# Scaling the inputs of the unit sums behind the root (second feed-forward) and in front of it (first), in a macaron block of 512 tokens on one core

## The chip, the cores and the metric

The kernel runs on one core of one Trainium2 chip. The metric is the device time of one launch in microseconds (us); less is better. The core has five engines with instruction streams of their own: TensorE (PE, matmuls; its weight loads are PEld), VectorE (DVE), ScalarE (ACT), GpSimd (POOL) and SyncE (SP, which here only issues transfers). They wait for each other through semaphores. Two on-chip memories matter: SBUF, and PSUM, into which TensorE writes.

## The reference

One layer in float32 on x of 512 tokens by 1024 features:

```
x = x + 0.5 * swiglu(rms_norm(x, ffn1_norm), ffn1_gate, ffn1_up, ffn1_down)
x = x + hybrid_mixer(rms_norm(x, mix_norm), ...)      # linear attention, differential attention, short convolution
x = x + 0.5 * swiglu(rms_norm(x, ffn2_norm), ffn2_gate, ffn2_up, ffn2_down)
out = rms_norm(x, final_norm)

rms_norm(x, g) = x * rsqrt(mean(x*x) + eps) * g
swiglu(h, wg, wu, wd) = (silu(h @ wg) * (h @ wu)) @ wd      # 1024 -> 2816 -> 1024
```

## The kernel before

**Layout and precision.** x lies with features on partitions, as KT = 8 tiles of 128 features by 512 tokens. Each matmul of float32 accuracy is three matmuls (`three`, L570): operands are split into a high part (`_hi`, written by ScalarE, `split_hi`, L1106) and a remainder (`_lo`, written by VectorE, `split_lo`, L1486, a subtraction of two SBUF operands), and hi x hi, hi x lo and lo x hi are added up. The rms factor is applied after the products: the matmuls work on x * gain, and the result is multiplied by `rinv`.

**Feed-forward.** The 2816 hidden features are 22 tiles (FT). The first four (PLAIN) are computed by plain products: `pair(m)` is a gate product and an up product, each of one weight slab of 128 x 1024 and 24 matmuls of 512 columns. The other 18 are "units" which use a Strassen-like scheme: seven block products of 256 columns on sums of weight quarters and on sums of activation quarters. The sums of the weights are GpSimd's, one unit after the other (`sums`, L483). The sums of the activations are made once per feed-forward, also by GpSimd (`activation_sums`, L505): six TENSOR_TENSOR instructions of 128 x 1024 on `xg`. `xg` is x * gain in plain float32, eight tiles written by ScalarE (`scaled_x`, L1125). ScalarE and VectorE then split the sums into `s_hi` and `s_lo`, in pair 2 and pair 3, and the first unit's products read them. `xg`, the sums and the squares of the start lie in parts of the array `h` that are not yet in use.

**The root.** For the norm, PE adds up the squares (`mean_squares`, L594, four small matmuls), ScalarE takes the square root (`root`, L1157), VectorE inverts it (`invert`, L1514: a reciprocal of four columns and four TENSOR_SCALARs of 128 columns that put it on the diagonal of `rinv`), PE spreads it over the partitions (`spread_rms`, L602, waits for `diag_ready`), and ScalarE copies the result from PSUM to `rinv` (`copy_rms`, L1161). In the first feed-forward (f = 0) the mean squares stand behind pair 1's gate product and the spread in the middle of pair 1's up product (`spread_at`, L630). In the second (f = 1) the mean squares stand between the two products of pair 0, and the spread behind them.

**Order.** Each engine's program is written out by hand; it runs in order and stops at the first wait that isn't met. In ScalarE's `pair(0)` stand: splits, the root, another split, the scalings of `xg` (k from 0 in the second feed-forward, from 4 in the first, where 0 to 3 stand ahead of `ffn_up`), the copy of the rms, then the wait for VectorE's first gate product and the Silu. In VectorE's `pair(0)` stand a split, the inversion, another split, then the wait for `rinv`, and the gate product. GpSimd's `activation_sums` begins with a wait for all eight tiles of `xg` (`xg_ready`). PE takes the slabs in order and waits for `lo_ready` of each. A slab's slot can be split again once PE has used it (`slab_used`) and be loaded again by SyncE once its remainder is made (`lo_ready`).

Of the kernel before, what the change touches and what calls it, by code (L numbers as in the profile page):

```python
# [33 lines left out]
KT = D // P  # L34
# [17 lines left out]
HK = KT // 2  # L52
# [37 lines left out]
UP2 = WO + KT  # L90
# [54 lines left out]
def half_tokens(c):  # L145
    return slice(c * HALF, (c + 1) * HALF)
# [6 lines left out]
def slab_width(s):  # L153

    if s < DN1 or WO <= s < DN2:
        return UPW
    if s < MX or s >= DN2:
        return len(down_tiles((s - DN1 if s < MX else s - DN2))) * P
    kind = MIX[s - MX]
    return UPW if kind[0] == "T" else kind[3] * NAT_W[kind[1]]  # L160
# [16 lines left out]
def build_layer(nc, xT, up_w, down_w, t_w, dv_w, nat_w, out_w, gains, gk_up, gk_bias, gla_gain, diff_gain,  # L177
                lam_qk, rel_bias, conv_w, onehot, decay_mats, level_masks, ident_c, out):
    tvec = nc.dram_tensor("bias_by_distance", (HEADS * COPIES, 5 * P), F32, kind="Internal")
    with ExitStack() as ctx:  # L180
# [3 lines left out]
        def sem(name):  # L184
            return ctx.enter_context(nc.semaphore(name))
# [119 lines left out]
        hi_ready, lo_ready, slab_used = sem("hi_ready"), sem("lo_ready"), sem("slab_used")  # L305
        x_updated, squared, sq_added = sem("x_updated"), sem("squared"), sem("sq_added")
# [58 lines left out]
        def slot(s):  # L365
            return s % 2

        def loads(s):

            return 16 * (s // 2)  # L370
# [87 lines left out]
        def _(pool):  # L458
# [46 lines left out]
            def activation_sums(f):  # L505

                a11, a21 = (xg[:, 0:HK, half_tokens(t)] for t in range(2))
                a12, a22 = (xg[:, HK:KT, half_tokens(t)] for t in range(2))
                s1, s2, s3, s4 = (s_raw[:, :, q, :] for q in (S1, S2, S3, S4))
                pool.wait_ge(xg_ready, KT * (f + 1))  # L510
                for n, (out_ap, in0, in1, op) in enumerate((
                        (s1, a22, a21, ALU.subtract), (s3, a11, a21, ALU.subtract), (s2, a11, a22, ALU.add),
                        (s4, a11, a12, ALU.subtract), (s2, a21, s2, ALU.subtract), (s4, s1, s4, ALU.add))):
                    if n >= 4:
                        pool.wait_ge(s_made, 6 * f + n - 1)
                    pool.tensor_tensor(out_ap, in0, in1, op).then_inc(s_made, 1)  # L516
# [586 lines left out]
        def _(act):  # L1103
            load_pieces(act, 0)

            def split_hi(s, n=0):  # L1106

                if isinstance(s, int) and s >= END:
                    return
                if not (isinstance(n, int) and (s + n < 3 or s >= END - 3)):  # L1110
                    act.wait_ge(slab_used, n + (s - 1))
                act.wait_ge(raw_loaded[slot(s)], 8 * n + loads(s))
                w = slab_width(s)
                dst = w_hi[:, slot(s), 0:w]
                if isinstance(s, int) and isinstance(n, int) and s >= END - 3:
                    k = KT * (s - (END - 3))
                    dst = last_hi[:, k:k + w // P, :].rearrange("p k c -> p (k c)")
                act.activation(dst, raw[:, slot(s), 0:w], ACT.Copy).then_inc(hi_ready, 1)  # L1118
# [6 lines left out]
            def scaled_x(gi, k):  # L1125
                act.activation(xg[:, k, :], x[:, k, :], ACT.Copy, scale=gain[:, gi, k:k + 1]).then_inc(xg_ready, 1)  # L1126
# [30 lines left out]
            def root(phase):  # L1157
                act.wait_ge(stat_ready, 2 * phase + 1)
                act.activation(rnat[:], ps[:, STAT, 0:NB], ACT.Sqrt, bias=eps_t[:]).then_inc(rms_ready, 1)

            def copy_rms(phase):  # L1161
                act.wait_ge(stat_ready, 2 * phase + 2)
                act.activation(rinv[:], ps[:, STAT, :], ACT.Copy).then_inc(rinv_ready, 1)

            def ffn_up(f, up0):
                gi = 2 * f

                def pair(m):
                    s = up0 + 2 * m
                    if m + f and not (m == 1 and f == 0):  # L1170
                        split_hi(s + 2)
                    if m == 0:
                        if f == 0:
                            split_hi(s + 3)
                        root(2 * f)
                        split_hi(s + (3 if f else 4))
                        for k in range(0 if f else HK, KT):
                            scaled_x(gi, k)
                        copy_rms(2 * f)
                    act.wait_ge(gate_scaled, PLAIN * f + m + 1)  # L1180
                    act.activation(gate_s[:, m % 2, :], gate_s[:, m % 2, :], ACT.Silu).then_inc(silu_done, 1)
                    if m and m < PLAIN - 1:
                        split_hi(s + 3)
                    if m == 2:
                        act.wait_ge(s_made, 6 * (f + 1))
                        for j in range(HK):
                            act.activation(s_hi[:, j, :, :], s_raw[:, j, :, :], ACT.Copy).then_inc(s_hi_ready, 1)
                    if m == PLAIN - 1:
                        ga(0, 0)
                        gb(0, 0)  # L1190

                def ga(i, b):

                    v = 2 * i + b
                    act.wait_ge(t2_ready, v + (FAST * f + 1))
                    if not (isinstance(i, int) and v + f == 0):
                        act.wait_ge(m5_done, v + FAST * f)
                    act.activation(sum_hi[:, GA, :], t_raw[:, GA, :], ACT.Copy).then_inc(ga_hi, 1)

                def gb(i, b):  # L1200
                    v = 2 * i + b
                    act.wait_ge(t3_ready, v + (FAST * f + 1))
                    if not (isinstance(i, int) and v + f == 0):
                        act.wait_ge(m7_done, v + FAST * f)
                    act.activation(sum_hi[:, GB, :], t_raw[:, GB, :], ACT.Copy).then_inc(gb_hi, 1)

                def take(q, i, b, bank, done, used):

                    v = 2 * i + b
                    act.wait_ge(done, v + (FAST * f + 1))  # L1210
                    if not (isinstance(i, int) and v + f == 0):
                        act.wait_ge(used, v + FAST * f)
                    act.activation(snap[:, q, :], ps[:, bank[b], 0:HALF], ACT.Copy).then_inc(snap_ready[q], 1)  # L1213

                def silu(i, b):
                    v = 2 * i + b
                    act.wait_ge(c11_scaled, v + (FAST * f + 1))
                    act.wait_ge(c21_scaled, v + (FAST * f + 1))
                    act.activation(gate_s[:, b, :], gate_s[:, b, :], ACT.Silu).then_inc(silu_done, 1)  # L1219

                def unit(i, b, prev):

                    v = 2 * i + b
                    s = up0 + 2 * PLAIN + b
                    if prev:
                        take(2, *prev, A_BANK, m7_done, c22_done)
                        gb(i, b)
                    if prev and isinstance(i, int) and v == FAST - 1:
                        split_hi(s + 2 * i + 1)
                    else:  # L1230
                        split_hi(s + 1, 2 * i)
                    take(0, i, b, A_BANK, m1_done, c11_added)
                    if prev:
                        silu(*prev)
                        act.wait_ge(m3_done, v + FAST * f)
                    act.wait_ge(t4_ready, v + (FAST * f + 1))
                    act.activation(sum_hi[:, GC, :], raw_u[:, b, :].rearrange("p (a c) -> p a c", a=2), ACT.Copy)\
                        .then_inc(gc_hi, 1)
                    take(1, i, b, A_BANK, m6_done, c12_done)
                    if not (isinstance(i, int) and v == FAST - 1):  # L1240
                        ga(*((i, 1) if b == 0 else (i + 1, 0)))

                for m in range(PLAIN):
                    pair(m)
                    if f == 0 and m == 2:
                        act.wait_ge(start_mm, 1)
                        act.activation(lam[:, 0:2], ps[:, 7, 0:2], ACT.Exp, scale=float(D)).then_inc(start_act, 1)
                unit(0, 0, None)
                unit(0, 1, (0, 0))
                with act.Fori(1, FAST // 2 - 1) as i:  # L1250
                    unit(i, 0, (i - 1, 1))
                    unit(i, 1, (i, 0))
                last = FAST // 2 - 1
                unit(last, 0, (last - 1, 1))
                unit(last, 1, (last, 0))
                take(2, last, 1, A_BANK, m7_done, c22_done)
# [915 lines left out]
```

## Time and profile before

| | |
|---|---|
| median of 3 runs | 952.75 us (952.41 to 953.43) |
| the profiled execution | 953.2 us |
| its span, first to last instruction | 951.4 us |
| PE busy | 941.7 us, 99% |
| DVE busy | 685.9 us, 72% |
| ACT busy | 435.9 us, 46% |
| POOL busy | 358.2 us, 38% |
| granted TensorE clock, mean | 1.000 of full speed (2.4 GHz) |

A busy PE here means that matmuls overlap: a matmul of 512 columns lasts 0.39 us in the trace, but the next starts 0.23 us after it. So short waits of PE are seen best in the distances between starts. In a timeline the columns are the start in us, the duration in us, engine, line of the kernel, operation, what it writes and reads, the shapes and the count; in brackets the idle time of that engine just before and what ended it.

### The profile page before, as it was taken

To read this page: it belongs to the slowest core of one execution; us is meant where nothing else is said; L and a number is where in the kernel's file an instruction comes from. 1 tells how busy PE (TensorE), PEld (TensorE's weight loads), DVE (VectorE), ACT (ScalarE), POOL (GpSimd) and SP (SyncE) were. 2 spreads that over 40 slices of the span, in tenths; PEclk is the share of its full clock that TensorE was granted. 3 is DMA by queue.
4 is the path that set the end of the run, shared out by engine and by line. 5 is a ranking of instruction groups with operands and counts; after the bars stand their busy time and mean duration, and the time that the engine had idled before them with its cause. 6 is when DMAs were issued, how large, how long until landed. Compare 5 with 4: busy or idle time off the path is not lost.

```text
span 951.4 us, 16549 instructions
## 1 busy us (share of the span) xinstructions
PE 941.7 (99%) x6290; PEld 843.0 (89%) x6290; DVE 685.9 (72%) x956; ACT 435.9 (46%) x686; POOL 358.2 (38%) x241
## 2 busy tenths in 40 slices
PE   9999999999999999999999999999999999999997
PEld 7899999999888889777899788889999999988887
DVE  6699999998543375677578964379999999833444
ACT  7565454556522233654534323544555555632331
POOL 0777777762010135110100015387767676000001
PEclk9999999999999999999999999999999999999999
DMA  6323333232222325222212123233242322232322
GB/s 211 117 105 109 112 95 125 88 131 71 90 100 100 104 79 170 75 74 78 72 57 68 46 88 106 71 133 112 89 132 88 125 96 98 80 100 77 102 99 89
DMA packets 31104, 94.27 MB, mean 99 GB/s; under 512 B 4464, under 2 KB 7712, under 8 KB 31056
## 3 DMA queue, kind: packets, MB, share of 16 engines
q1 hardware_dynamic: 29120, 90.28, 28.8%
q0 software_dynamic: 1648, 3.07, 1.3%
q8 instruction: 33, 0.54, 0.2%
q10 hardware_dynamic: 288, 0.26, 0.1%
q14 instruction: 15, 0.12, 0.0%
HBM read 90.38 MB, written 2.42 MB: 98 GB/s over the span
## 4 chain that ended last, share of the span: by engine, by line
PE 86%; DVE 6%; POOL 2%; ACT 2%; issue 1%; DMA 1%; SPq 0%; DVEq 0%; ACTq 0%; POOLq 0%
PE ps L572 27%; PE ps L574 26%; PE ps L573 26%; POOL h L516 2%; DVE w_lo L1496 1%; DVE s_lo L1553 1%; PE ps L851 1%; PE ps L931 1%; PE ps L872 1%; PE ps L904 1%; ACT h L1126 1%; DVE states L1883 1%; ACT w_hi L1118 1%; DMA x<-xT 0%; PE ps L861 0%
## 5 line engine op out<-in xcount | busy, mean ns | idle before, releaser
L1496 DVE TENSOR_TENSOR w_lo<-raw,w_hi 128x1024 fp32r<-128x1024 f32 (+2 forms) x128 | 195.9, 1530 | 146.0 <-ACT w_hi L1118 146.0
L1118 ACT ACTIVATE w_hi<-raw 128x1024 fp32r<-128x1024 f32 (+2 forms) x128 | 131.3, 1026 | 193.1 <-PE ps L574 193.1
L572 PE MATMUL ps<-xg_hi,w_hi 128*128 128x256 f32 (+1 forms) x528 | 178.2, 338 | 0.8 <-DVE w_lo L1496 0.6
L574 PE MATMUL ps<-xg_hi,w_lo 128*128 128x256 f32 (+1 forms) x528 | 175.0, 331 | 0.0
L573 PE MATMUL ps<-xg_lo,w_hi 128*128 128x256 f32 (+1 forms) x528 | 174.8, 331 | 0.0
L572 PE MATMUL ps<-s_hi,sum_hi 128*128 128x256 f32 x576 | 160.1, 278 | 1.2 <-ACT snap L1213 0.9
L573 PE MATMUL ps<-s_lo,sum_hi 128*128 128x256 f32 x576 | 159.4, 277 | 0.0
L574 PE MATMUL ps<-s_hi,sum_lo 128*128 128x256 f32 x576 | 159.2, 276 | 0.0
L573 PE MATMUL ps<-h_lo,w_hi 128*128 128x512 f32 x330 | 128.4, 389 | 0.0
L572 PEld LDWEIGHTS ps<-xg_hi,w_hi 128*128 128x128 f32 x528 | 99.9, 189 | 19.1 <-issue 8.2
L572 PEld LDWEIGHTS ps<-s_hi,sum_hi 128*128 128x128 f32 x576 | 108.3, 188 | 2.0 <-issue 1.7
L574 PEld LDWEIGHTS ps<-xg_hi,w_lo 128*128 128x128 f32 x528 | 99.9, 189 | 9.9
L573 PEld LDWEIGHTS ps<-s_lo,sum_hi 128*128 128x128 f32 x576 | 108.3, 188 | 0.0
L574 PEld LDWEIGHTS ps<-s_hi,sum_lo 128*128 128x128 f32 x576 | 108.2, 188 | 0.0
L573 PEld LDWEIGHTS ps<-xg_lo,w_hi 128*128 128x128 f32 x528 | 99.9, 189 | 8.5
L574 PE MATMUL ps<-h_hi_s,w_lo 128*128 128x512 f32 x240 | 93.4, 389 | 0.0
L572 PE MATMUL ps<-h_hi_s,w_hi 128*128 128x512 f32 x240 | 93.4, 389 | 0.0
L491 POOL TENSOR_TENSOR t_raw<-raw,raw_u 128x512 f32<-128x512 f32 x36 | 54.9, 1526 | 79.5 <-DMA raw_u<-up_w 68.5
L495 POOL TENSOR_TENSOR t_raw<-raw_u 128x512 f32<-128x512 f32 x36 | 79.6, 2212 | 0.0
L502 POOL TENSOR_TENSOR raw_u<-t_raw,raw 128x512 f32<-128x512 f32 x36 | 71.9, 1998 | 11.5 <-POOL t_raw L498 7.0
L573 PEld LDWEIGHTS ps<-h_lo,w_hi 128*128 128x128 f32 x330 | 62.0, 188 | 12.6
L1219 ACT ACTIVATE gate_s<-gate_s 128x512 f32<-128x512 f32 x34 | 21.5, 634 | 110.5 <-DVE gate_s L1582 110.5
(255 smaller groups left out, 1891.5 us busy)
## 6 DMA issues: line engine op xcount, KB each, us to landing
raw<-up_w SPq DMA_DIRECT2D x50, 512.0 KB, 4.1
raw<-down_w SPq DMA_DIRECT2D x38, 512.0 KB, 3.2
raw_u<-up_w SPq DMA_DIRECT2D x36, 512.0 KB, 3.2
raw<-t_w SPq DMA_DIRECT2D x15, 512.0 KB, 3.2
raw<-out_w SPq DMA_DIRECT2D x8, 512.0 KB, 3.2
raw<-nat_w SPq DMA_DIRECT2D x4, 576.0 KB, 3.8
x<-xT SPq DMA_DIRECT2D x8, 256.0 KB, 4.8
out<-x SPq DMA_DIRECT2D x8, 256.0 KB, 2.2
```

The lines of the kernel that those rows point to most:

```text
L491: pool.tensor_tensor(t_raw[:, T1, :], raw[:, slot(s), 0:HW], raw_u[:, b, 0:HW], ALU.add)\
L495: pool.tensor_tensor(t_raw[:, T3, :], raw_u[:, b, 0:HW], raw_u[:, b, HW:UPW], ALU.add)\
L502: pool.tensor_tensor(raw_u[:, b, 0:HW], t_raw[:, T2, :], raw[:, slot(s), HW:UPW], ALU.add)\
L516: pool.tensor_tensor(out_ap, in0, in1, op).then_inc(s_made, 1)
L572: pe.matmul(out_ap, a[0], b[0], start=first, stop=False, skip_group_check=resumed)
L573: pe.matmul(out_ap, a[0], b[1], start=False, stop=False, skip_group_check=resumed)
L574: return pe.matmul(out_ap, a[1], b[0], start=False, stop=last, skip_group_check=resumed)
L851: last = pe.matmul(ps[:, 4 + mp, 0:w], dqk[r, h % 2, 0, i * P:(i + 1) * P], dqk[r, h % 2, 1, 0:w], start=True, stop=True)
L872: last = pe.matmul(ps[:, 7, 0:DV], pT[:, n % 2, b * P:(b + 1) * P], dv[:, b, h * DV:(h + 1) * DV], start=b == 0, stop=b == i)
L1118: act.activation(dst, raw[:, slot(s), 0:w], ACT.Copy).then_inc(hi_ready, 1)
L1219: act.activation(gate_s[:, b, :], gate_s[:, b, :], ACT.Silu).then_inc(silu_done, 1)
L1496: dve.tensor_tensor(lo, raw[:, slot(s), 0:w], hi, ALU.subtract).then_inc(lo_ready, 1)
```

## The change

Two edits. On ScalarE, in `pair(0)`: in the first feed-forward the scalings of tiles 4 to 7 now stand in front of the root, and the split of slab 4 behind it; in the second, the eight scalings stand right behind the root, with a wait for `slab_used` at UP2 in front of them (PE is through with the slabs before the second feed-forward), and in front of the split of slab UP2 + 3. On GpSimd: in the first feed-forward the sums also wait for `sq_added` at 8 (the start's squares lie in places that the sums overwrite).

```
@@ GpSimd, activation_sums
                 pool.wait_ge(xg_ready, KT * (f + 1))
+                if f == 0:
+                    pool.wait_ge(sq_added, KT)
                 for n, (out_ap, in0, in1, op) in enumerate((
...
@@ ScalarE, ffn_up, pair(m)
                     if m == 0:
                         if f == 0:
                             split_hi(s + 3)
-                        root(2 * f)
-                        split_hi(s + (3 if f else 4))
-                        for k in range(0 if f else HK, KT):
-                            scaled_x(gi, k)
+                            for k in range(HK, KT):
+                                scaled_x(gi, k)
+                            root(0)
+                            split_hi(s + 4)
+                        else:
+                            root(2)
+                            act.wait_ge(slab_used, UP2)
+                            for k in range(KT):
+                                scaled_x(gi, k)
+                            split_hi(s + 3)
                         copy_rms(2 * f)
```

## Rows read from the trace of the kernel before

**Rows 1.** The page, part 1: busy time, share of the span, instructions.
```profile
PE 941.7 (99%) x6290; PEld 843.0 (89%) x6290; DVE 685.9 (72%) x956; ACT 435.9 (46%) x686; POOL 358.2 (38%) x241
```
**Rows 2.** Timeline of PE, at the gaps of both stages.
```profile
27.51 1.05 PE L606 MATMUL ps<-rinv,ones 128*128 128x128 f32 x8
28.32 0.48 PE L572 MATMUL ps<-xg_hi,w_hi 128*128 128x512 f32 x1
...
36.36 0.39 PE L574 MATMUL ps<-xg_hi,w_lo 128*128 128x512 f32 x1
36.83 0.50 PE L572 MATMUL ps<-xg_hi,w_hi 128*128 128x512 f32 x1
...
53.61 0.39 PE L574 MATMUL ps<-xg_hi,w_lo 128*128 128x512 f32 x1
54.41 0.36 PE L572 MATMUL ps<-xg_hi,w_hi 128*128 128x256 f32 x1 [0.40 <-DVE w_lo L1496]
...
57.74 0.36 PE L572 MATMUL ps<-s_hi,sum_hi 128*128 128x256 f32 x1 [0.23 <-issue]
...
619.33 0.39 PE L574 MATMUL ps<-xg_hi,w_lo 128*128 128x512 f32 x1
619.91 0.50 PE L572 MATMUL ps<-xg_hi,w_hi 128*128 128x512 f32 x1 [0.19 <-DVE w_lo L1496]
```
**Rows 3.** Timeline of ACT, around the roots of both feed-forwards.
```profile
21.37 1.04 ACT L1118 ACTIVATE w_hi<-raw 128x1024 fp32r<-128x1024 f32 x1
24.83 0.26 ACT L1159 ACTIVATE rnat<-ps,eps_t 128x4 f32<-128x4 f32 x1 [2.42 <-PE ps L598]
...
25.94 2.55 ACT L1126 ACTIVATE h<-x,gain 128x512 f32<-128x512 f32 x4
...
602.38 0.27 ACT L1159 ACTIVATE rnat<-ps,eps_t 128x4 f32<-128x4 f32 x1 [0.17 <-PE ps L598]
607.95 1.06 ACT L1118 ACTIVATE w_hi<-raw 128x1024 fp32r<-128x1024 f32 x1 [5.31 <-PE ps L574]
608.92 5.00 ACT L1126 ACTIVATE h<-x,gain 128x512 f32<-128x512 f32 x8
613.83 0.57 ACT L1163 ACTIVATE rinv<-ps 128x512 f32<-128x512 f32 x1
```
**Rows 4.** Timeline of DVE: first feed-forward, and the final norm.
```profile
25.34 0.88 DVE L1519 TENSOR_SCALAR rinv<-ident,rnat 128x128 f32<-128x128 f32 x4
26.13 1.22 DVE L1496 TENSOR_TENSOR w_lo<-raw,w_hi 128x1024 fp32r<-128x1024 f32 x1
...
34.19 2.59 DVE L1496 TENSOR_TENSOR w_lo<-raw,w_hi 128x1024 fp32r<-128x1024 f32 x1 [0.20 <-ACT w_hi L1118]
...
938.58 0.42 DVE L1725 TENSOR_TENSOR x<-x,rinv 128x256 f32<-128x256 f32 x1 [2.86 <-ACT rinv L1151]
938.92 0.95 DVE L1725 TENSOR_TENSOR x<-x,rinv 128x256 f32<-128x256 f32 x1
```
**Rows 5.** Timeline of POOL: all six sums, then single ones.
```profile
28.57 16.17 POOL L516 TENSOR_TENSOR h<-h 128x1024 f32<-128x1024 f32 x6 [27.54 <-ACT h L1126]
...
33.29 2.40 POOL L516 TENSOR_TENSOR h<-h 128x1024 f32<-128x1024 f32 x1
35.66 3.38 POOL L516 TENSOR_TENSOR h<-h 128x1024 f32<-128x1024 f32 x1
```
**Rows 6.** TENSOR_SCALAR by source line: count, min/median/max ns, first and last start.
```profile
L1519 DVE TENSOR_SCALAR rinv<-ident,rnat x12: 280/283/290, 25.3 to 604.2; 128x128 f32<-128x128 f32 x12
...
L1924 DVE TENSOR_SCALAR shared<-tv,convw x1: 486/486/486, 534.2 to 534.2; 128x512 f32<-128x512 f32 x1
```
**Rows 7.** PE's first and last matmuls; one window with the granted clock.
```profile
1.01 5.47 PE L834 MATMUL ps<-ones 128*128 128x128 f32 x28 [1.01 <-POOL one_t L482]
...
942.00 1.27 PE L797 MATMUL ps<-ones 128*128 128x128 f32 x10
...
945.26 0.71 PE L802 MATMUL ps<-rinv,ones 128*128 128x128 f32 x4
...
950.50:951.40 0.90, 0.00 (x0) 0.00 (x0) 0.00 (x0) 0.00 (x0) 0.00 (x0) 0.72 0.01 1
```

## The prediction

> **What bounds the kernel now.** I read the page first: PE is busy 941.7 of 951.4 us, nothing else above 72% [rows 1]. On an engine that full, a change helps only where PE stands still, and hurts wherever it makes PE wait. So the second view was PE's timeline at both stages the diff touches, and I looked for starts further apart than the usual 0.23 us (512 columns) or 0.12 us (256 columns).
>
> Four places are in reach of the change [rows 2]. At 36.36 the next matmul starts 0.47 later: 0.24 lost. At 53.61 it starts 0.80 later: 0.57 lost, put down to DVE's w_lo. At 57.74 a wait of 0.23. In the second feed-forward 619.33 to 619.91: 0.35 lost, w_lo again. Sum 1.39 us. The first matmul behind a gap also takes 0.50 where others take 0.39, about 0.1 more at each: **at most 1.8 us to be won** in the whole kernel by earlier sums.
>
> Third view: ScalarE, VectorE and GpSimd in the same stretches [rows 3 to 5]. In the first feed-forward ScalarE splits slab 3 at 21.37, stands still until PE's mean squares are there, takes the root at 24.83, splits slab 4 and then scales xg tiles 4 to 7 (25.94 for 2.55, to 28.49). GpSimd starts its six sums 0.08 later, at 28.57, and ends at 44.74. Between root and those scalings VectorE inverts the root: four TENSOR_SCALARs of 128 columns from 25.34 for 0.88, to 26.22. PE needs them at its spread (L606) at 27.51, in the middle of slab 3's product: 1.3 us of slack, **with GpSimd idle all the while**. In the second feed-forward the root is at 602.38, the eight scalings at 608.92 for 5.00, the copy of the spread rms behind them at 613.83.
>
> **The change, second feed-forward.** Nothing is added but one wait (slab_used at UP2), which PE met before it began the product that runs when the root is taken; behind it on ScalarE stand the eight scalings, and it costs nothing. The scalings start at 602.38 + 0.27 = 602.65 and end by 607.65, inside the 5.31 us of idleness in front of the split of UP2 + 3 at 607.95, which waits for PE. GpSimd can start at 607.7 in place of 614.0, the copy at about 608.95 in place of 613.83, so VectorE's first gate product, the Silu and the split in front of slab 4 move up by up to 5 us, until PE's own products hold them. The split that PE waited for at 619.91 can then end about 2 us earlier even if it waits for a GpSimd sum: gain 0.35 + 0.11 = 0.46. VectorE's inversion comes behind the root, with at most a split of 1.2 in front of its 1.1 us (24.83 + 0.26 to 26.22 in the first stage), so by 605; GpSimd starts only at 607.7: no meeting. The six sums end 6.3 us earlier, but the next thing GpSimd wants is the unit's raw slabs, whose loads hang on a split that PE releases; I give that nothing, and 0 to 0.5 either way.
>
> **First feed-forward.** The four scalings move in front of the root: 21.37 + 1.04, less the 0.1 by which two ScalarE instructions overlap, + 2.55 = 24.87 (24.96 at most). The root still goes at 24.83 to 24.9, slab 4's split behind it, the copy of the rms where it was: ScalarE has lost nothing. GpSimd's added wait (sq_added 8) is for VectorE's start sums, which PE's mean squares needed before the root of 24.83 could go; queued behind are only its own sums. No DMA is moved past another. GpSimd starts at 24.95 in place of 28.57. Were that all, the three stalls of the first feed-forward would shrink, at most by 0.24 + 0.57 + 0.23 + 0.3 = 1.34.
>
> **But this start is 0.4 us ahead of VectorE's four TENSOR_SCALARs, which stood in front of it before.** GpSimd and VectorE exclude each other in this trace [rows 4, 5]. A split (L1496) of 1024 columns takes 1.22 at 26.13 with GpSimd idle; the one at 34.19 takes 2.59: GpSimd's sum from 33.29 ends at 35.69, and VectorE ends 1.09 later. GpSimd's next sum, started at 35.66, takes 3.38 where the one before took 2.40: it waited for VectorE in its turn. And they take turns instruction by instruction, also when VectorE's are small and need no semaphore between them: L1725 at 938.58 takes 0.42, the next, at 938.92, 0.95.
>
> The rows show that only for TENSOR_TENSOR with two SBUF operands; no TENSOR_SCALAR of the trace runs beside a GpSimd sum. So the price has two ends. Low end: it isn't held, price 0. High end: each of the four waits for one sum. GpSimd's pitch is 35.66 - 33.29 = 2.37, a TENSOR_SCALAR's (0.88 - 0.28) / 3 = 0.20. First sum 24.95 to 27.32; then 4 x 0.20 of VectorE with 3 x 2.37 of GpSimd between them: done at 27.32 + 0.80 + 7.11 + 0.1 = **35.3** in place of 26.2. PE stands from 27.5 to 35.4: **7.9 us**. A middle: the first one waits, the other three slip through together: 27.32 + 0.88 = 28.2, a stall of 0.7 and 0.1 of restart.
>
> Which end? TENSOR_SCALAR takes 486 ns for 512 columns and 283 for 128 [rows 6], 0.53 ns a column; TENSOR_TENSOR 1.22 for 1024 and 0.42 for 256, 1.04 ns a column. It moves two words at once, as a TENSOR_TENSOR with two SBUF operands does, and that kind waits. I take the high end, as the nearest rows in kind (L1725, back to back, 256 columns) are at it.
>
> The Trainium skill (SBUF — State Buffer, Who interferes with whom) says the same of more kinds: copy, cast and tensor_scalar in a two-port mode hold the port pair shared with GpSimd, whoever issues first has it for the whole instruction, the other blocks. For TENSOR_TENSOR the trace agrees (2.59 against 1.22); for tensor_scalar no run here shows it yet. By that rule the sum is the high end's, without it the low end's.
>
> **The clock.** At the end of the trace the last matmuls are over at 945.97, and the mean granted clock of 950.50 to 951.40 is 0.72 [rows 7]: half for 0.50 us, so it fell some 4.9 us after PE went idle. PE would be idle 7.8 us here, so I expect a fall to the 1.2 GHz level. At the start 28 matmuls of 128 columns take 5.47; ten warm ones take 1.27. With 0.11 each warm, 0.22 at half clock, (5.47 - 0.28) = 0.22 n + 0.11 (27 - n) gives n = 20, 4.4 us at half, 2.2 us lost. Price of the restart 2.2, between 0 (no fall) and 3.3 (half as long again).
>
> **Sum.** +7.9 +2.2; and with PE 10 us late, the stalls at 36.4, 53.6, 57.7 and 619.9 are covered: -1.8. Slab 4's split waits for another sum behind the inversion (35.3 + 2.4 + 1.1 = 38.8); PE, with twelve matmuls of 0.23 left of slab 3 behind 28.32, asks for it at 31.0 + 10.1 = 41.1, so it is covered. Net +8.3 on the profiled execution's 953.2, which is 0.45 above the median: 961.5 profiled, **961.0** beside the median of 952.75. Its own range: 958.7 (no clock fall, 0.3 less else) to 962.8 (3.3 of it, 0.4 more stall).
>
> **Rivals.**
> 1. *TENSOR_SCALAR is not held.* Then only the early sums count. For: no row shows it held. Against: its rate. The best is -1.8; GpSimd's raw slabs still come at PE's pace, so some of the wait at 57.74 stays, -1.5: 951.2. This is the rival on the other side; it decides at the four instructions at 25.3 alone, and its price is 7.9 + 2.2 less.
> 2. *Held once.* The first waits for the first sum, the rest go through (their pitch of 0.20 is shorter than their 0.28, so the next is issued before the last is done). For: that overlap. Against: L1725 overlaps too (0.34 pitch, 0.42 each) and still alternates. +0.8 - 1.5 = -0.7: 952.0.
> 3. *The full stall, but the clock stays up.* For: the fall came only 4.9 us into idleness, and once. Against: 7.8 is well over it. 961.0 - 2.2 = 958.8.
> 4. *The second part gives nothing or the sums' earlier start costs it.* GpSimd then holds VectorE during the split of slab 3 at 609 (needed at 614): hidden. At worst the 0.46 is not won: +0.5 on any case.
>
> **How the numbers follow.** Full stall with the clock's fall 0.57, full stall without 0.12, two or three of the four held 0.04, held once 0.07, not held 0.17, something else 0.03. A measurement tells about 0.2% (1.9 us) from no change. Slower: 0.73. Not held lies at -1.5, just inside 0.2%, with a third of its chance beyond: faster 0.07. Same: the rest of it, held once and half of the unknown, 0.20. As the cases of slower hold only three quarters, the range reaches over the others: 950.9 to 963.0.
>
> **What would show it.** L606 of the first feed-forward at about 35.4 in place of 27.5, with a wait on DVE rinv L1519; L1519 of some 2.2 to 2.6 us each in place of 0.28; six GpSimd sums from 24.95 to about 40; a granted clock under 1.00 between 31 and 40 and 512-column matmuls 0.45 apart behind it; later no gap at 36.4, 53.6 and 619.9 (shifted by the delay). L1126 at 22.3 and, with its eight, at 602.6. I am wrong if L1519 keeps 0.28 beside a running L516 (rival 1), or if only the first is long (rival 2), or if the clock stays at 1.00 (rival 3).

## The result and the profile after

The changed kernel takes **961.9 us** (median of 6 runs, 960.63 to 962.2), the one before 953.01 (6 runs, 952.4 to 953.43): ratio 1.0091 [1.008, 1.0102]. It is slower, by 8.9 us, and within the predicted range for the forecast's own case (958.7 to 962.8). The profiled execution took 962.2, its span is 960.4: 9.0 longer than before.

The page, part 1, and the clock line of part 2 (40 slices of 24 us, tenths of full speed):

```profile
PE 944.6 (98%) x6290; PEld 845.5 (88%) x6290; DVE 693.0 (72%) x956; ACT 435.7 (45%) x686; POOL 355.5 (37%) x241
...
PEclk9799999999999999999999999999999999999999
```

The second slice is at 7 tenths, all others at 9, which stands for 90% or more. Against [rows 1]: PE's busy time grew by 2.9 us with the same 6290 matmuls, so some of them ran slower, and the rest of the 9.0 is standing still. VectorE is busy for 7.1 us more with the same 956 instructions: a busy engine here also means one that is held. Where, the timeline of PE shows, beside [rows 2]:

```profile
27.65 0.39 PE L576 MATMUL ps<-xg_hi,w_lo 128*128 128x512 f32 x1
34.90 2.07 PE L608 MATMUL ps<-rinv,ones 128*128 128x128 f32 x8 [6.86 <-DVE rinv L1527]
36.62 0.77 PE L574 MATMUL ps<-xg_hi,w_hi 128*128 128x512 f32 x1
37.19 0.63 PE L575 MATMUL ps<-xg_lo,w_hi 128*128 128x512 f32 x1
...
40.61 0.41 PE L574 MATMUL ps<-xg_hi,w_hi 128*128 128x512 f32 x1
...
41.33 0.39 PE L574 MATMUL ps<-xg_hi,w_hi 128*128 128x512 f32 x1
```

The spread that started at 27.51 starts at 34.90, behind the inversion (its TENSOR_SCALARs are L1527 here, L1519 before). The matmuls behind it are 0.43 apart instead of 0.23, until 40.6. Slab 4's first one is at 41.33. Windows of the same stretch (length, then busy time and instructions of PE, PEld, DVE, ACT and POOL, then the granted clock, DMA share, GB/s):

```profile
28.00:30.00 2.00, 0.04 (x1) 0.00 (x0) 2.00 (x1) 0.00 (x0) 2.00 (x1) 1.00 0.00 0
30.00:31.00 1.00, 0.00 (x0) 0.00 (x0) 1.00 (x2) 0.00 (x0) 1.00 (x2) 0.71 0.00 0
31.00:34.00 3.00, 0.00 (x0) 0.00 (x0) 3.00 (x2) 0.00 (x0) 3.00 (x2) 0.50 0.00 0
...
40.00:41.00 1.00, 1.00 (x4) 0.77 (x4) 0.93 (x2) 0.03 (x1) 0.38 (x1) 0.67 0.78 315
```

The clock halves in 30 to 31 (a mean of 0.71 is half speed for the last 0.58 us, so from 30.42, 2.4 after the last matmul's end at 28.04) and is back at 40.66, by the same working. The 1.2 GHz level holds from the spread's start for 5.8 us, half of which is lost. VectorE and GpSimd, beside [rows 4, 5], taken in windows so short that each instruction has its own row:

```profile
25.56 0.18 DVE L1525 RECIPROCAL rnat<-rnat 128x4 f32<-128x4 f32 x1 [1.38 <-ACT rnat L1161]
25.77 2.17 DVE L1527 TENSOR_SCALAR rinv<-ident,rnat 128x128 f32<-128x128 f32 x1
27.87 2.37 DVE L1527 TENSOR_SCALAR rinv<-ident,rnat 128x128 f32<-128x128 f32 x1
30.16 2.38 DVE L1527 TENSOR_SCALAR rinv<-ident,rnat 128x128 f32<-128x128 f32 x1
32.46 2.38 DVE L1527 TENSOR_SCALAR rinv<-ident,rnat 128x128 f32<-128x128 f32 x1
34.76 3.39 DVE L1504 TENSOR_TENSOR w_lo<-raw,w_hi 128x1024 fp32r<-128x1024 f32 x1
```
```profile
25.46 2.40 POOL L518 TENSOR_TENSOR h<-h 128x1024 f32<-128x1024 f32 x1 [24.44 <-ACT h L1128]
27.83 2.33 POOL L518 TENSOR_TENSOR h<-h 128x1024 f32<-128x1024 f32 x1
30.12 2.33 POOL L518 TENSOR_TENSOR h<-h 128x1024 f32<-128x1024 f32 x1
...
37.03 3.35 POOL L518 TENSOR_TENSOR h<-h 128x1024 f32<-128x1024 f32 x1
```

The first TENSOR_SCALAR starts 0.31 us after a sum, the others 0.04 after, and each ends 0.08 to 0.09 after that sum's end: each has waited for one. A kind that took 0.28 takes up to 2.38. ScalarE is where the prediction put it, beside [rows 3]:

```profile
22.83 2.55 ACT L1128 ACTIVATE h<-x,gain 128x512 f32<-128x512 f32 x4
25.28 0.24 ACT L1161 ACTIVATE rnat<-ps,eps_t 128x4 f32<-128x4 f32 x1
...
611.28 0.26 ACT L1161 ACTIVATE rnat<-ps,eps_t 128x4 f32<-128x4 f32 x1 [0.17 <-PE ps L600]
611.44 5.00 ACT L1128 ACTIVATE h<-x,gain 128x512 f32<-128x512 f32 x8
```

In the second feed-forward, the place where the unit products begin, before (first fence, not among the rows above) and after (second):

```profile
633.40 5.70 DVE L1553 TENSOR_TENSOR s_lo<-h,s_hi 128x1024 fp32r<-128x1024 f32 x3
633.97 1.80 POOL L491 TENSOR_TENSOR t_raw<-raw,raw_u 128x512 f32<-128x512 f32 x1 [2.82 <-issue]
```
```profile
616.52 17.13 POOL L518 TENSOR_TENSOR h<-h 128x1024 f32<-128x1024 f32 x6 [6.39 <-ACT h L1128]
641.50 1.54 POOL L491 TENSOR_TENSOR t_raw<-raw,raw_u 128x512 f32<-128x512 f32 x1 [7.85 <-issue]
641.79 6.79 DVE L1561 TENSOR_TENSOR s_lo<-h,s_hi 128x1024 fp32r<-128x1024 f32 x3
...
653.28 0.28 PE L576 MATMUL ps<-xg_hi,w_lo 128*128 128x256 f32 x1
653.79 0.36 PE L574 MATMUL ps<-s_hi,sum_hi 128*128 128x256 f32 x1 [0.23 <-issue]
```

GpSimd's first sum of weights now starts 0.29 us ahead of VectorE's first `s_lo`, where it stood 0.57 behind it. So all three `s_lo` are held by it and its successors (6.79 against 5.70), the split behind them is late, and PE has two gaps that it did not have: one at 653.28 and, not shown, one of 0.23 at 650.01. A third, 1.0 at 676.40, is as it was in before (667.36 to 668.50).

For the accounts below the time of PE is cut at five starts. Each number is the difference of two starts, in us; the first is the distance from the last matmul of the product to the spread, less the usual 0.23. The last column ends where the last group of matmuls starts (945.26 in before).

| kernel | stall before the first spread | spread to slab 4 | slab 4 to the mixer's spread | mixer's spread to the second feed-forward's | from there to the last group |
|---|---|---|---|---|---|
| before | 0.01 | 3.64 | 335.48 | 241.12 | 337.51 |
| after | 7.02 | 6.43 | 334.22 | 241.13 | 337.56 |
| first part alone | 7.53 | 5.66 | 334.30 | 241.12 | 337.45 |
| second part alone | 0.00 | 3.64 | 335.50 | 241.13 | 337.64 |
| sums behind the inversion | 0.00 | 3.64 | 335.03 | 241.13 | 337.64 |
| identity in PSUM | 0.01 | 3.64 | 334.88 | 241.14 | 337.56 |
| one instruction | 0.94 | 3.77 | 334.34 | 241.11 | 337.41 |
| half sums | 2.98 | 5.09 | 334.31 | 241.11 | 337.56 |
| kept warm | 7.84, of it 6.42 filled by the extra matmuls | 3.75 | 334.27 | 241.18 | 337.50 |
| weight sum behind the first s_lo | 0.01 | 3.63 | 335.55 | 241.12 | 336.95 |
| early splits | 0.01 | 3.64 | 334.78 | 241.11 | 335.36 |
| early splits, identity in PSUM | 0.01 | 3.64 | 334.42 | 241.12 | 335.31 |

After against before: +7.0 + 2.8 - 1.3 + 0.0 + 0.05, and the stretch ahead of the spread is 0.4 longer (the last matmul before it starts at 27.65 against 27.27, in a part of the program that is unchanged). That is the 9.0.

### The profile page after: what moved, and what is told of

Its sections match the earlier page's. It is cut to its first block, busy times and chain, and to the rows that moved or that the text cites. A ratio compares the mean times of both kernels' runs of the same rounds, so it can differ in the third digit from the quotient of the medians.

```text
span 960.4 us, 16550 instructions
## 1 busy us (share of the span) xinstructions
PE 944.6 (98%) x6290; PEld 845.5 (88%) x6290; DVE 693.0 (72%) x956; ACT 435.7 (45%) x686; POOL 355.5 (37%) x241
## 4 chain that ended last, share of the span: by engine, by line
PE 88%; DVE 6%; ACT 2%; issue 1%; DMA 1%; SPq 1%; POOL 1%; DVEq 0%; ACTq 0%; POOLq 0%
PE ps L574 28%; PE ps L576 27%; PE ps L575 27%; PE ps L853 1%; DVE w_lo L1504 1%; PE ps L933 1%; PE ps L874 1%; DVE s_lo L1561 1%; DVE rinv L1527 1%; PE ps L906 1%; DVE states L1891 1%; DMA raw<-up_w 1%; ACT w_hi L1120 1%; ACT h L1128 0%; PE ps L863 0%
## 5 line engine op out<-in xcount | busy, mean ns | idle before, releaser
L1504 DVE TENSOR_TENSOR w_lo<-raw,w_hi 128x1024 fp32r<-128x1024 f32 (+2 forms) x128 | 192.7, 1506 | 146.6 <-ACT w_hi L1120 146.5
```

The lines of the kernel that those rows point to most:

```text
L1504: dve.tensor_tensor(lo, raw[:, slot(s), 0:w], hi, ALU.subtract).then_inc(lo_ready, 1)
```

## The experiments

The theory: the four TENSOR_SCALARs of the first inversion each wait for one of GpSimd's sums, because both engines want the same access to SBUF; PE stands for that time, and the clock falls while it stands. The rivals were that the loss sits in the second feed-forward, that it is ScalarE's new order in the first rather than the meeting of the two engines, and that the clock costs nothing. The kernel before ran beside all of them: 952.87 beside experiments 1 to 4, 953.01 beside 5 to 8, 952.86 beside the last two.

**1 and 2. Each part alone.** The first keeps only the first feed-forward's new order, the second only the second's:

```
first_only, second feed-forward:       second_only, first feed-forward:
  root(2)                                root(0)
  split_hi(s + 3)                        split_hi(s + 4)
  for k in range(KT):                    for k in range(HK, KT):
      scaled_x(gi, k)                        scaled_x(gi, k)
```

> The first feed-forward's part of the change alone; the second feed-forward keeps its old order. Theory (turns): the whole loss lies at the four TENSOR_SCALARs of the first inversion, so this kernel shows it all: about +8.9 us on before (961.9), L1519's instructions at some 2.3 us each, PE waiting about 7 us for diag_ready, the clock at half until about 40. Rival (second part pays too, because the sums' earlier end there meets VectorE's s_lo): if the second part costs, this kernel is faster than the full change, by up to 0.6 us; if the second part gains its 0.46, it is slower by as much.

> The second feed-forward's part alone (eight scalings right behind the root); the first keeps its old order. Theory (given back): the stall in front of slab 4 (0.35 plus 0.11 of restart) goes, but GpSimd's first weight sum now starts just ahead of VectorE's three s_lo instead of 0.6 behind the first of them, all three are held, and the split of the first unit's slab ends about 1 us later against PE: new gaps of about 0.3 and 0.5. Sum within 0.3 us of before, 952.8 to 953.3. Rival (my forecast of the second part): the 0.46 stays won, 952.5. Neither can be told from before by the total alone; the gaps in PE's timeline tell them apart.

The first alone: 961.11, ratio 1.009 [1.0075, 1.0106]. The second alone: 953.1, ratio 1.0001 [0.9992, 1.001]. The loss is the first part's. Its median is 0.8 under the full change's, but the clock accounts for that and not the second part. The runs of both kernels fall into two groups by their mean granted clock: at 0.995 they took 960.63 and 961.0 (full) and 960.85, 960.99 and 961.23 (first part), at 0.994 they took 961.9 to 962.2 (full) and 962.79 (first part). So the clock's share of the loss differs by about 1 us from run to run. The second part gives nothing: it takes away the gap in front of slab 4, and gives the same back at the first unit. Its trace has the order of the changed kernel again, GpSimd 0.30 us ahead:

```profile
632.57 1.54 POOL L491 TENSOR_TENSOR t_raw<-raw,raw_u 128x512 f32<-128x512 f32 x1 [7.84 <-issue]
632.87 2.33 DVE L1561 TENSOR_TENSOR s_lo<-h,s_hi 128x1024 fp32r<-128x1024 f32 x1
```

PE loses 0.22 at 641.1 and 0.39 at 644.4, where 0.3 and 0.5 were expected.

**3. The sums behind the inversion.** The full change, but GpSimd starts when the inversion is done; ScalarE's order stays.

```
 if f == 0:
     pool.wait_ge(sq_added, KT)
+    pool.wait_ge(diag_ready, 1)
```

> The full change, with one wait more: in the first feed-forward GpSimd's sums also wait for diag_ready, so for VectorE's inversion. Theory (turns): all of the loss goes. L1519 is back at 0.28 each, PE does not wait at the spread, the sums start at about 26.3, 2.3 us before those of before, and the stalls at 53.6 and 57.7 shrink by about 0.6 to 1.2 together: 951.7 to 952.6. Rival (something in the reordered ScalarE program costs, say the later root): it stays well above 955.

952.24, ratio 0.9995 [0.9986, 1.0004], the clock at 1.00 throughout:

```profile
25.64 0.88 DVE L1528 TENSOR_SCALAR rinv<-ident,rnat 128x128 f32<-128x128 f32 x4
26.70 16.98 POOL L519 TENSOR_TENSOR h<-h 128x1024 f32<-128x1024 f32 x6 [25.68 <-DVE rinv L1528]
```

Moving the six sums back by 1.24 us takes away all of the 8.9. ScalarE's new order costs nothing; the meeting was the cost. Against the second part alone the first part now gains 0.47 of span (335.50 to 335.03). It does not come from where it was expected: the gap in front of slab 5 is gone (it was at 36.3 in the second part alone, 0.35 with the longer first matmul), the one at 53.6 is only 0.08 smaller and the one at 57.7 as it was.

**4. Early splits.** Experiment 3, and in the second feed-forward the sums' own splits (`s_hi` on ScalarE, all four `s_lo` on VectorE) stand ahead of the split of slab 7.

```
 ScalarE, pair(2):
-    split_hi(s + 3)
+    if not f: split_hi(s + 3)
     act.wait_ge(s_made, 6 * (f + 1))
     for j in range(HK): ... s_hi
+    if f: split_hi(s + 3)
 VectorE, pair(2), behind split_lo(s + 2):
+    if f:
+        for j in range(HK): sums_lo(j)        # and none of them later
```

> As sums_behind_inversion, and in the second feed-forward ScalarE and VectorE split the activation sums in the idle time that the earlier sums open: s_hi and s_lo right behind the split of slab 6, in front of slab 7's. Theory (the chain of s_lo, unit split and sum_lo in VectorE's queue sets the four later gaps of the second feed-forward): the gaps at the first unit and the one of 0.85 us at ACT snap go too, 1.2 to 2.2 us under sums_behind_inversion: 949.8 to 951.2. Rival (the late gap of 0.85 comes from GpSimd and the raw_u loads alone, not from VectorE's backlog): it stays, and only 0.4 to 0.8 is won.

**949.96** (949.12 to 950.48), ratio 0.9969 [0.9958, 0.998]: faster than both kernels, and 2.3 under experiment 3, a little more than the 1.2 to 2.2 expected. The second feed-forward is 2.3 us shorter than in experiment 3 (337.64 to 335.36), and PE has no gap left there. In experiment 3 its starts show 0.23 at 640.1, 0.40 at 643.4 and 1.00 at 666.5, behind a snapshot by ScalarE (L1222), together 1.6; the rest is the longer first matmul behind each and intervals under 0.08. The six sums' early end is used here for the first time: the four `s_lo` run undisturbed at 1.16 each and are done 0.2 us before GpSimd's first weight sum begins.

```profile
626.63 4.63 DVE L1567 TENSOR_TENSOR s_lo<-h,s_hi 128x1024 fp32r<-128x1024 f32 x4 [0.24 <-ACT s_hi L1196]
631.48 1.29 POOL L491 TENSOR_TENSOR t_raw<-raw,raw_u 128x512 f32<-128x512 f32 x1 [7.85 <-issue]
```

**5. One instruction for four.** If each instruction waits for one sum, one instruction of 512 columns waits once.

```
-for b in range(NB):
-    dve.tensor_scalar(rinv[:, b * P:(b + 1) * P], ident[:], rnat[:, b:b + 1], float(D), mult, mult)
+dve.scalar_tensor_tensor(rinv as (b t), ident broadcast over b, float(D), rnat broadcast over t, mult, mult)
```

> The full change, but the inversion puts the diagonal down with one instruction of 512 columns (SCALAR_TENSOR_TENSOR with two broadcast SBUF operands) in place of four TENSOR_SCALARs of 128. Theory (turns): one instruction waits for one sum only. It ends at about 27.9 + 0.7 = 28.5, PE stands about 0.7 to 1.0 us in place of 7.0, the clock stays at 1.00: 952.0 to 953.0. Rival (VectorE is slowed in proportion to its work while GpSimd runs, 0.88 us became 9): the one instruction takes 6 to 9 us as well and the time stays at 960 or more.

952.41, ratio 0.9994 [0.9985, 1.0004]. PE waits 0.78 us, and the clock stays at 1.00:

```profile
25.46 2.63 DVE L1526 SCALAR_TENSOR_TENSOR rinv<-ident,rnat 128x512 f32<-128x512 f32 x1
```
```profile
25.15 2.39 POOL L518 TENSOR_TENSOR h<-h 128x1024 f32<-128x1024 f32 x1 [24.12 <-ACT h L1128]
27.50 2.83 POOL L518 TENSOR_TENSOR h<-h 128x1024 f32<-128x1024 f32 x1
```

The price goes with the number of VectorE's instructions, not with their columns: the same 512 columns wait once and end at 28.09 instead of 34.84. The kind of instruction changed too, but this one is held as well, by one sum; only the number of waits fell.

**6. Half sums.** The other side of the same product: each sum cut in two of 512 columns, so that each of the four waits for half as long.

```
+for c in range(2):
+    j = slice(c * HK // 2, (c + 1) * HK // 2)
+    last = pool.tensor_tensor(out_ap[:, j], in0[:, j], in1[:, j], op)
-pool.tensor_tensor(out_ap, in0, in1, op)
```

> The full change, with each of GpSimd's six activation sums cut into two of 512 columns. Theory (turns): each TENSOR_SCALAR waits for one GpSimd instruction, and these are half as long, so about 1.2 us each: the inversion ends near 30.7, PE stands 2.5 to 3.2 us, and the clock most likely stays up or falls only for a moment. Total 955 to 957.5. Rival (slowed in proportion to work): the inversion is as long as with whole sums, 9 us, and the total stays at 961 to 962.

956.45, ratio 1.0032 [1.0022, 1.0043]. The last three TENSOR_SCALARs take 1.30 to 1.33 and each ends 1.22 to 1.25 behind the one before; PE waits 2.83:

```profile
27.85 1.30 DVE L1530 TENSOR_SCALAR rinv<-ident,rnat 128x128 f32<-128x128 f32 x1
```
```profile
28.00:30.00 2.00, 0.00 (x0) 0.00 (x0) 2.00 (x2) 0.00 (x0) 2.00 (x2) 0.97 0.00 0
30.00:32.00 2.00, 1.57 (x7) 1.57 (x8) 2.00 (x2) 0.00 (x0) 2.00 (x3) 0.50 0.00 0
32.00:34.00 2.00, 2.00 (x9) 1.67 (x8) 1.29 (x2) 1.44 (x2) 2.00 (x2) 0.68 0.22 53
```

The clock fell here too, in a wait of 2.8 us: a mean of 0.97 over 28 to 30 is half speed for the last 0.12, from 29.88, 2.3 after the last matmul's end at 27.61; by the last row it was back at 33.28. It seems not to fall in every run, though. In three of the nine runs the mean granted clock was 0.999, as in the kernel before, and these took 954.67 to 955.47; in the other six it was 0.996 or 0.997, and they took 956.43 to 957.99.

**7. The identity in PSUM.** What do the two engines exclude each other over? PE writes the identity into a free part of PSUM, and the four TENSOR_SCALARs of the first inversion read it there. GpSimd starts as early as in the changed kernel.

```
+pe.matmul(ps[:, 5, 0:P], ident[:], ident[:], start=True, stop=True)      # ahead of the mean squares
-dve.tensor_scalar(rinv[...], ident[:], rnat[...], ...)
+dve.tensor_scalar(rinv[...], (ps[:, 5, 0:P] if phase == 0 else ident[:]), rnat[...], ...)
```

> The full change, but in the first feed-forward the four TENSOR_SCALARs read the identity from PSUM (PE puts it there with one extra matmul) in place of SBUF. Theory (what is shared between VectorE and GpSimd is the second access to SBUF, which a TENSOR_SCALAR with its source in PSUM does not use): they run at about 0.28 each beside the running sums, PE does not wait, the clock stays up: 951.2 to 952.5. Rival (any VectorE instruction that touches SBUF waits for GpSimd): 2.3 us each, as in the full change, 961 to 962.

952.16, ratio 0.9991 [0.9981, 1.0001]. In the middle of a running sum the four take 0.35 or 0.34 each; the subtraction of two SBUF operands right behind them is held:

```profile
25.18 1.13 DVE L1530 TENSOR_SCALAR rinv<-ps,rnat 128x128 f32<-128x128 f32 x4
26.22 2.13 DVE L1507 TENSOR_TENSOR w_lo<-raw,w_hi 128x1024 fp32r<-128x1024 f32 x1
```
```profile
24.87 2.41 POOL L518 TENSOR_TENSOR h<-h 128x1024 f32<-128x1024 f32 x1 [23.84 <-ACT h L1131]
```

So the TENSOR_SCALAR is held only when the 128 x 128 identity comes from SBUF; an output and a scalar of each partition in SBUF are not enough. Whether it is then the second read or a second write that waits, these runs do not separate. By the Trainium skill (VectorE: DVE Perf Modes, Mode 2×_2P) a TENSOR_SCALAR in float32 reads through both of VectorE's read ports when its source is in SBUF, and cannot from PSUM; these runs agree: 0.28 us from SBUF with GpSimd idle, 0.34 from PSUM beside it, 2.38 from SBUF beside it.

**8. Kept warm.** The changed kernel with 28 extra matmuls of 128 columns, whose result nobody reads, in PE's wait.

```
 if phase == 0:
+    for _ in range(28):
+        pe.matmul(ps[:, 5, 0:P], ones[:], ones[:], start=True, stop=True)
 pe.wait_ge(diag_ready, phase + 1)
```

> The full change, with 28 more matmuls of 128 columns (ones by ones, float32, result not used, about 6.2 us) in PE's wait for the first inversion. The wait of about 7 us stays, PE is busy in it. Theory (a fall of the clock is part of the loss): the granted clock stays at 1.00 and 2.3 to 2.8 us of the 8.9 come back: 959.1 to 959.6. Rival (the half clock costs nothing, since PE's lateness is covered elsewhere): the total stays within 0.5 us of 961.9.

959.61, ratio 1.0067 [1.005, 1.0084]. The clock is at 1.00 in every window from 28 to 40, and the spread takes 1.16 instead of 2.07 (a matmul of this kind leaves two records: 56 for the 28, 8 for the spread's four):

```profile
27.22 6.42 PE L608 MATMUL ps<-ones 128*128 128x128 f32 x56
35.05 1.16 PE L611 MATMUL ps<-rinv,ones 128*128 128x128 f32 x8 [1.42 <-DVE rinv L1530]
```

Of the 8.9, 2.3 (961.9 - 959.6) is the clock; in the traces 6.43 - 3.75 = 2.7 from the spread to slab 4.

**9. The weight sum behind the first `s_lo`.** Is the second part's lost gain really the order of the two engines at 641.5? The second part alone, with GpSimd's first weight sum held until one `s_lo` is made.

```
+if f == 1 and b == 0 and i == 0:
+    pool.wait_ge(s_lo_ready, HK + 1)
 pool.wait_ge(raw_loaded[slot(s)], 16 * i + loads(s))
```

> As second_only, but in the second feed-forward GpSimd's first weight sum also waits for the first s_lo (s_lo_ready). Theory (turns, in the second part): in second_only GpSimd starts that sum 0.3 us ahead of VectorE's three s_lo and all three are held, 6.8 us together; with the sum behind the first one only two are held, 5.7 us as in the kernel before, and the gap of about 0.4 that second_only has at the first unit shrinks to 0.2 or less, the one in front of slab 4 stays away. Total 0.3 to 0.5 us under second_only and under before: 952.3 to 952.7. Rival (the unit's chain is set by GpSimd's three weight sums, which now end later): the gap stays at 0.4 or grows, and the total is 953.0 or more.

952.53, ratio 0.9995 [0.9986, 1.0005], against 952.86 beside it. Both gaps at the first unit are gone; in the spans that stretch is 0.69 shorter than with the second part alone (337.64 to 336.95):

```profile
632.47 4.60 DVE L1563 TENSOR_TENSOR s_lo<-h,s_hi 128x1024 fp32r<-128x1024 f32 x3
633.76 2.21 POOL L493 TENSOR_TENSOR t_raw<-raw,raw_u 128x512 f32<-128x512 f32 x1 [9.44 <-DVE s_lo L1563]
```

Only one of the three is held, where two were expected: they take 1.22, 1.22 and 2.32, together 4.60 and not 5.7. GpSimd's weight sum starts 1.2 us later (633.76 against 632.57), at no price that shows. The times alone do not separate this kernel from the one before (the interval holds 1); the gaps in the trace do.

**10. Early splits with the identity in PSUM.** Experiment 4 with the collision avoided by experiment 7's way instead of GpSimd's wait.

> early_splits with the identity of the first inversion in PSUM in place of GpSimd's wait for the inversion. Theory: the sums of the first feed-forward start at about 24.9 in place of 26.6, the two gaps that early_splits still has at the first unit (0.25 and 0.39) go as in identity_in_psum, where a gap of 0.42 at 36 came in: net 0.1 to 0.6 us better, 949.3 to 949.9, at best hardly to be told from early_splits. Rival (the gap at 36 eats it all): 950.0.

950.05, ratio 0.997 [0.9959, 0.9981]: the same as experiment 4 within what can be measured. The sums start earlier, but the split of slab 5 then falls beside one of them (2.99 us from 34.03), and the gap that follows, 0.63 lost at 36.2, eats what they bring. The first feed-forward is only 0.36 shorter than in experiment 4 (334.42 against 334.78), and the medians don't show that.

## Why the prediction was right

**The full stall: right in kind, 0.9 too large.** The step was: four TENSOR_SCALARs, each held by one sum, PE until 35.4. Measured 34.90, and 7.0 us of stall against 7.9. The waits alternate one to one, as taken from the final norm's TENSOR_TENSORs [rows 4]; experiments 3, 5, 6 and 7 each change one factor of the product and find the price that follows (0, one wait, half, 0). The size was off in the round. I had added VectorE's 0.20 to GpSimd's 2.37; a round in the trace is 2.30 (25.46... 27.83, 30.12), less than a sum's pitch alone. Three rounds of 2.57 became three of 2.30, that is 0.8. That the sums began at 25.46 and not at 24.95 hardly enters: PE's last matmul in front of the spread was 0.4 later too. GpSimd paid nothing for these small instructions that waited for it; only a long one (3.39 at 34.76) holds it in turn, as in [rows 5].

**Rivals 1 and 2** (not held, held once) are refuted by the four rows of 2.17 to 2.38. The reason that decided, that TENSOR_SCALAR moves two words at once and so resembles the kind that waits, is borne out by experiment 7: with the source in PSUM it is not held. The Trainium skill (SBUF — State Buffer, Who interferes with whom), quoted with the prediction for tensor_scalar, agrees with the trace now (2.38 against 0.28), as does its remark that the order of issue decides who blocks: GpSimd issued 0.31 us before VectorE and was never held by these four.

**The clock: right, 2.8 against 2.2**, within the 0 to 3.3 given. Rival 3 (no fall) is refuted by the windows and by experiment 8. The reason given for it was weak, though. I read one fall, 4.9 us after the last matmul, and said the stall was well over that. The clock fell 2.4 us after PE's last matmul here, 2.3 with half sums, and 4.6 in the first part alone, whose windows are:

```profile
31.00:32.00 1.00, 0.00 (x0) 0.00 (x0) 1.00 (x1) 0.00 (x0) 1.00 (x1) 0.98 0.00 0
...
38.00:39.00 1.00, 1.00 (x4) 0.77 (x3) 0.61 (x2) 0.99 (x2) 1.00 (x1) 0.60 0.01 4
```

That is down at 31.96 and back at 38.80. From the spread's start it stayed down for 5.8, 2.9 and 4.1 us, and the second stretch of the table grew by 2.8, 1.45 and 2.0, half of each. One reading of the fall said little of the next; the 0 to 3.3 given as bounds held all three. The upper end of the forecast's range, 962.8, does not follow from its terms (961.0 + 1.1 + 0.4 = 962.5); the measured 961.9 lies below both.

**The covered stalls of the first feed-forward: right.** Predicted 0.24 + 0.57 + 0.23 + 0.3 = 1.34, measured 335.48 - 334.22 = 1.26. With PE 10 us late the gaps at 36.4 and 53.6 are gone; where the one at 57.7 was, starts 0.16 late are left of 0.40. Experiments 3 and 7 show what early sums would bring without the delay: 0.45 to 0.6. Rival 1's price of 951.2 counted 1.5; the closest kernel to it, experiment 7, took 0.85 less than before.

**The second feed-forward: wrong by 0.5, rival 4 in its place.** The gap at 619.9 went as predicted, and 0.46 with it. The step that failed is "the six sums end 6.3 us earlier, but the next thing GpSimd wants is the unit's raw slabs ...; I give that nothing, and 0 to 0.5 either way". Those slabs came early enough to move GpSimd's first weight sum by 0.86 us against VectorE (from 0.57 behind to 0.29 ahead), and that was enough to turn the order, hold three `s_lo` instead of two and cost the 0.5 again: gaps of 0.23 and 0.40, with 0.1 for the longer matmul behind, stand against the 0.46 won and the 0.26 of two small ones that shrank (at 644.6 and 657.3 in before). Net +0.05. Experiment 9 shows that this order is the cause of the gaps.

Where the 0.86 comes from, the traces show as well, though no releaser is named for GpSimd's start ("issue"). The last of the unit's slabs is loaded by SyncE (`raw_u`, L401) right behind a load that waits for VectorE's split of slab 6. Before, and (second fence) after:

```profile
626.82 2.09 DVE L1496 TENSOR_TENSOR w_lo<-raw,w_hi 128x1024 fp32r<-128x1024 f32 x1 [0.41 <-ACT w_hi L1118]
629.30 0.43 SPq L401 DMA_DIRECT2D raw_u<-up_w  x1
```
```profile
635.21 1.23 DVE L1504 TENSOR_TENSOR w_lo<-raw,w_hi 128x1024 fp32r<-128x1024 f32 x1 [0.40 <-ACT w_hi L1120]
636.84 0.43 SPq L401 DMA_DIRECT2D raw_u<-up_w  x1
```

From the start of that split to VectorE's first `s_lo` it is 6.58 us in both. From its end to the issue of the load it is 0.4 in both, and from there to GpSimd's first weight sum 4.67 (633.97) and 4.66 (641.50). What changed is the split itself: a sum held it in before (2.09), none does now (1.23), as the sums end earlier. That is the 0.86. The loads do hang on a split, as the prediction said, but on one that the six sums had held.

So the sum of +8.3 met +9.0 by errors that partly cancel: -0.9 (stall), +0.6 (clock), +0.1 (covered stalls), +0.5 (second part), +0.4 (the start of the program, which differs from run to run). That the total came so close is luck; that the stall and the fall of the clock make it up is not.

## What to carry to other kernels

Before moving work of GpSimd, look for rows of short VectorE instructions of the kinds that waited here (TENSOR_SCALAR with its source in SBUF, TENSOR_TENSOR with two SBUF operands) that will run beside it: the price is the number of those instructions times the length of one GpSimd instruction, however few columns VectorE's have. It can be avoided by fewer VectorE instructions (952.41 here), a source in PSUM (952.16) or GpSimd's start a microsecond later (952.24), which cannot be told apart by their times; shorter GpSimd instructions (956.45) help in part. The later start needs only one wait. A gain that appears as an earlier start is only worth something where the next consumer is moved up with it, as the early splits did; alone, it turned an order of two engines by 0.3 us somewhere else and was lost.

## What the runs showed of the hardware that was not expected

- A RECIPROCAL of four columns, SBUF to SBUF, takes 0.18 us beside a running sum (25.56, the sum from 25.46) and is not held.
- Turn-taking was free for GpSimd beside the four short instructions: a pitch of 2.30 while one of them waits in between, 2.37 without. It was not beside longer ones: the sum at 27.50 of experiment 5 took 2.83, the one at 37.03 of the changed kernel 3.35.
- One SCALAR_TENSOR_TENSOR of 512 columns with two broadcast SBUF operands ends 0.55 us after the sum that held it (28.09 against 27.54), while four TENSOR_SCALARs of 128 take 0.88.
- The clock fell between 2.3 and 4.6 us after the last matmul in front of the spread, and came back 2.9 to 5.8 us after the spread's start, in three kernels that differ little in this stretch. In experiment 5, with a wait of 0.78, it stayed up. At the end of the program the fall came 4.9 us after the last matmul in before, and 2.0 in experiment 5 (945.48 to 947.52, by a mean of 0.76 over 947 to 948).
